# Attention of a gated linear mixer between the tiles of a projection, and modulation rows fetched tile by tile

## The reference

```python
# modulation: nine vectors of 1024 per layer
mod = c_act @ mod_w[l] + mod_b[l]
# gated linear mixer, layer 0 of the second block
xa, ga, q, k, v, g, za = split(u @ w_in)
ya = rg_lru(causal_conv(xa)) * gelu(ga)
log_alpha = log_sigmoid(za @ gla_wa2 + gla_ba) / 16
bc = cumsum(log_alpha over each chunk of 64 tokens)
q_dec, k_inv, k_end = q * exp(bc), k * exp(-bc), k * exp(b_last - bc)
scores = tril(q_dec @ k_inv.T)                    # inside a chunk
state = decay * state + k_end.T @ v               # from chunk to chunk
o = scores @ v + q_dec @ state
yb = rms_norm(o, gla_norm_g) * silu(g)
out = concat(ya, yb) @ w_out
```

## Time and profile before

| what | value |
|---|---|
| median of 3 runs | 3293.67 us (3288.68 to 3298.96) |
| the profiled execution | 3289.53 us, span 3287.7 us, mean granted PE clock 0.957 |
| busy: PE / DVE / ACT / POOL | 3010.6 / 1896.7 / 564.0 / 197.4 us |
| p2, 16 tiles | 2281.3 to 2336.5 us of the span |
| attention, outside of dense tiles | 2336.5 to 2399.0 us |
| pout | 2399.0 to 2456.1 us |
| small FFN without rows, first product to last | 211.6 us (2469.3 to 2680.9) |
| the four with rows | 218.6, 213.8, 214.1, 215.8 us |

### The profile page before, as it was taken

The page is one execution under the profiler, slowest core; times in us unless marked ns, Lnnn a source line. Parts: engine busy times, 40 slices in busy tenths (PEclk is TensorE's granted clock), DMA queues, the critical chain, the costliest instruction groups (busy, mean ns, idle before and its releaser), DMA issues.

```text
span 3287.7 us, 60931 instructions
## 1 busy us (share of the span) xinstructions
PE 3010.6 (92%) x26800; PEld 2580.0 (78%) x26800; DVE 1896.7 (58%) x3378; ACT 564.0 (17%) x1284; POOL 197.4 (6%) x315
## 2 busy tenths in 40 slices
PE   7999999777878899999899999999889999989998
PEld 6444444666667699999789999988769989976898
DVE  1777666543445377677547767744126656633674
ACT  1000001343233210100221010024101011022201
POOL 0000000331143000000000000000000000000000
PEclk8999999898999999999999999999799999998999
DMA  5668995101200446556424655634333535521453
GB/s 216 236 230 326 373 339 201 40 4 58 86 16 4 167 154 225 198 206 220 151 94 165 199 198 181 203 100 128 102 103 129 174 127 175 174 74 59 146 182 101
DMA packets 362050, 514.85 MB, mean 157 GB/s; under 512 B 10865, under 2 KB 349873, under 8 KB 352193
## 3 DMA queue, kind: packets, MB, share of 16 engines
q1 hardware_dynamic: 350992, 364.11, 34.2%
q0 software_dynamic: 10224, 144.18, 11.2%
q10 hardware_dynamic: 576, 2.75, 0.2%
HBM read 509.97 MB, written 1.05 MB: 155 GB/s over the span
## 4 chain that ended last, share of the span: by engine, by line
PE 81%; DMA 7%; DVE 4%; ACT 4%; issue 2%; POOL 1%; SPq 0%; DVEq 0%; ACTq 0%; POOLq 0%
PE PS L2424 25%; PE PS L2464 14%; PE PS L580 9%; PE PS L2354 7%; PE PS L2374 5%; PE PS L600 5%; PE PS L752 4%; DMA W<-in_ffn_w_gu 3%; PE PS L2333 2%; PE PS L2475 2%; DMA ADAW<-in_ada_rows 2%; DVE ADAW L2655 1%; PE PS L1327 1%; PE PS L1421 1%; PE PS L1552 1%
## 5 line engine op out<-in xcount | busy, mean ns | idle before, releaser
L2424 PE MATMUL PS<-Y,W 128*128 128x128 f32 x4928 | 594.9, 280 | 56.5 <-ACT Y L2577 32.0
L2424 PEld LDWEIGHTS PS<-Y,W 128*128 128x128 f32 x4928 | 577.3, 196 | 64.2 <-issue 34.4
L2424 PE MATMUL PS<-Y,ARENA 128*128 128x128 f32 x3696 | 438.7, 275 | 0.0
L2424 PEld LDWEIGHTS PS<-Y,ARENA 128*128 128x128 f32 x3696 | 426.0, 192 | 0.0
L2354 PE MATMUL PS<-Y,W 128*128 128x512 f32 x704 | 303.8, 594 | 2.2 <-DVE Y L2877 2.2
L2464 PE MATMUL PS<-ARENA,W 128*128 128x128 f32 x2464 | 286.1, 275 | 1.3 <-DVE ARENA L2761 0.7
L2464 PEld LDWEIGHTS PS<-ARENA,W 128*128 128x128 f32 x2464 | 280.2, 192 | 2.7 <-DVE ARENA L2761 2.7
L2354 PEld LDWEIGHTS PS<-Y,W 128*128 128x128 f32 x704 | 134.2, 191 | 171.0 <-issue 170.5
L2655 DVE SCALAR_TENSOR_TENSOR ADAW<-ADAW,CB 128x1024 f32<-128x1024 f32 x200 | 238.5, 1220 | 27.4 <-DMA ADAW<-in_ada_rows 27.0
L580 PE MATMUL PS<-Y,W 128*128 128x256 f32 (+2 forms) x816 | 184.8, 390 | 21.6 <-DMA W<-in_o_w_in 11.1
L580 PEld LDWEIGHTS PS<-Y,W 128*128 128x128 f32 (+2 forms) x816 | 157.3, 194 | 48.8 <-DMA W<-in_o_w_in 11.5
(11 more groups left out here) (395 smaller groups left out, 3617.7 us busy)
## 6 DMA issues: line engine op xcount, KB each, us to landing
ADAW<-in_ada_rows POOLq DMA_DIRECT2D x68, 2048.0 KB, 8.9
W<-in_ffn_w_gu SPq DMA_DIRECT2D x88, 1024.0 KB, 7.8
W<-in_ffn_in SPq DMA_DIRECT2D x88, 1024.0 KB, 7.6
W<-in_ffn_w_down SPq DMA_DIRECT2D x32, 1408.0 KB, 10.5
W<-in_ffn_out SPq DMA_DIRECT2D x32, 1408.0 KB, 8.6
W<-in_even_w_in SPq DMA_DIRECT2D x40, 512.0 KB, 4.7
W<-in_e_w_in SPq DMA_DIRECT2D x34, 512.0 KB, 4.7
ARENA<-in_ada_columns SPq DMA_DIRECT2D x4, 2048.0 KB, 24.9
```

Of the source, the lines that this page charges most:

```text
L2424: last = mm(block_bank(b, q), w[left][:, k, q * P:(q + 1) * P], YB[right][:, k], start=(k == 0 and p not in (2, 5)), stop=(k == 3), skip_g ...
```

## The change

In the gla mixer:
- The attention has its own counters (s_gm products done, s_ge products read, s_gz parts of Z16 ready) and its own banks 4 to 7 (`gbank`).
- p2 does the Gelu gates first. Its 16 tiles are written out one by one, and parts of the attention follow single tiles, by the table `beside`: scores and transposes after tile 0, the states of heads 0 to 3 after tiles 2 to 5, two outputs each after tiles 6 to 9, the two sums of squares after tiles 10 and 11. The square is done in two halves, the roots after tiles 11 and 12.
- ACT does the exponentials after value tile 4 (they stood after value tile 7) and the root of TH after the first p2 tile (it stood after value tile 6).
- DVE does the cumulative sums and differences ahead of TH, then the decayed q and k, then the RG-LRU product and scans, and doesn't wait for p2 before the attention.
- pout waits part by part for Z16: one count for the first eight blocks, then one for each of the others.
- ST lies where QG, KG and LA lay, RR where XAP and TH lay.

In the FFNs: a list `fetch` spreads the four tiles of each row group over the chunks from the one after group g-2's use up to the one ahead of its own. POOL issues each tile as a DMA of 0.5 MB (`row_tile`) when the chunk's products begin. The first two groups of F[1] and all groups before them are fetched whole, as before. `ada` waits for the sum of the four.

```diff
@@ in gla_phases, pe
-                proj_pe(pe, mm, m["p2"], lambda i: lambda k: Y[:, k, 0:S])
...
+                def tile(i):
+                    c, idx = sec["w0"] + i // 2, sec["t0"] + i
+                    pe.wait_ge(s_w[c % 2], 32 * (c // 2 + 1))
+                    pe.wait_ge(s_ev, idx - 3)
...
+                def scores():
+                    pe.wait_ge(s_xr, n_qk)
...
+                def states(h):
+                    pe.wait_ge(s_ge, G_ST)
                     for par in range(2):
-                        pe.wait_ge(s_ev, idx - 3)
+                        j = G_ST + 2 * h + par
+                        if j > 3:
+                            pe.wait_ge(s_ge, j - 3)
...
+                def output(i):
+                    j = G_OUT + i
+                    h, q = i // 2, i % 2
+
+                    pe.wait_ge(s_ge, max(G_ST + 2 * (h + 1), j - 3))
...
+                def square_sums(g):
+                    j = G_SQ + g
+                    pe.wait_ge(s_ga, squared + g)
+                    pe.wait_ge(s_ge, j - 3)
...
+                beside = {0: [(scores, ()), (keys_turned, ())], 2: [(states, (0,))], 3: [(states, (1,))],
+                          4: [(states, (2,))], 5: [(states, (3,))], 6: [(output, (0,)), (output, (1,))],
+                          7: [(output, (2,)), (output, (3,))], 8: [(output, (4,)), (output, (5,))],
+                          9: [(output, (6,)), (output, (7,))], 10: [(square_sums, (0,))], 11: [(square_sums, (1,))]}
+                for i in range(16):
+                    tile(i)
+                    for part, args in beside.get(i, ()):
+                        part(*args)
+                pe.wait_ge(s_ev, m["p2"]["t1"])
...
+                    for k in range(16):
+                        if i == 0 and k in (0, *range(DT, 16)):
+                            pe.wait_ge(s_gz, max(1, k - DT + 2))
@@ in gla_phases, act
-                    elif i == 6:
-                        act.wait_ge(s_xr, n_th)
-                        A(TH, TH, ACT.Sqrt).then_inc(s_ga, 1)
-                    elif i == 7:
+                    elif i == 4:
                         act.wait_ge(s_xr, n_be)
                         A(QD, BC, ACT.Exp)
...
+                    elif i == 8:
+                        act.wait_ge(s_xr, n_th)
+                        A(TH, TH, ACT.Sqrt).then_inc(s_ga, 1)
+                    elif i == 18:
+                        for g in range(2):
+                            act.wait_ge(s_ge, G_SQ - 4 + 4 * g)
+                            A(AI[:, 4 * g:4 * g + 4], AR_[:, 4 * g:4 * g + 4], ACT.Square).then_inc(s_ga, 1)
+                    elif i in (19, 20):
+                        g = i - 19
+                        act.wait_ge(s_gm, G_SQ + g + 1)
...
@@ in gla_phases, dve
-                dve.wait_ge(s_ga, 6)
-                link(V.tensor_scalar(YH, TH, 1.0, None, ALU.add))
-                link(V.reciprocal(YH, YH))
-                say(V.scalar_tensor_tensor(TH, TH, 2.0, YH, ALU.mult, ALU.mult), n_th)
...
-                dve.wait_ge(s_ga, 8)
+                dve.wait_ge(s_ga, 6)
+                link(V.tensor_scalar(YH, TH, 1.0, None, ALU.add))
+                link(V.reciprocal(YH, YH))
+                say(V.scalar_tensor_tensor(TH, TH, 2.0, YH, ALU.mult, ALU.mult), n_th)
+                dve.wait_ge(s_ga, 9)
+                V.tensor_tensor(QD, QD, QG, ALU.mult)
+                V.tensor_tensor(KI, KI, KG, ALU.mult)
+                say(V.tensor_tensor(KE, KE, KG, ALU.mult), n_qk)
+                link(V.memset(SCO, 0.0))
+                dve.wait_ge(s_ga, 10)
                 link(V.tensor_tensor(AI, AI, TH, ALU.mult))
                 for f in range(DT):
                     ins = V.tensor_tensor_scan(XC[:, f], AR_[:, f], AI[:, f], 0.0, ALU.mult, ALU.add)
...
-                dve.wait_ge(s_ev, m["sc"])
-                link(V.tensor_tensor(Z16[:, 0:DT], Z16[:, 0:DT], XC, ALU.mult))
...
+                dve.wait_ge(s_ev, m["p2"]["t0"] + DT)
+                V.tensor_tensor(Z16[:, 0:DT], Z16[:, 0:DT], XC, ALU.mult).then_inc(s_gz, 1)
+                dve.wait_ge(s_ga, squared + 3)
                 link(V.reciprocal(RR, RR))
...
                 for i in range(DT):
+                    dve.wait_ge(s_ev, m["p2"]["t0"] + DT + i + 1)
+                    V.scalar_tensor_tensor(Z16[:, 8 + i], AR_[:, i], vec("gla_norm_g_2", i % 2), Z16[:, 8 + i],
+                                           ALU.mult, ALU.mult).then_inc(s_gz, 1)
@@ ahead of the phases, and in POOL's program
+        chunk_uses = [used for sec in F[1:] for used in sec["groups"]]
+        used_in = [u for u, used in enumerate(chunk_uses) if used]
+        fetch = [[] for _ in chunk_uses]
+        for g, last in enumerate(used_in[2:], 2):
+            free_at = used_in[g - 2] + 1
+            for i in range(GROUP):
+                fetch[free_at + i * (last - free_at) // GROUP].append((F[1]["group0"] + g, i))
...
+            def row_tile(g, i):
+                pool.wait_ge(s_acc, g - 1)
+                pool.dma_start(ADAW[:, g % 2, i], t["ada_rows"][g * P:(g + 1) * P, i * D:(i + 1) * D])\
+                    .then_inc(s_adaw[g % 2], 16)
+
             def small_ffn(sec):
-                for g in range(sec["group0"] + 2, min(sec["group0"] + sum(sec["groups"]) + 2, len(ADA_GROUPS))):
-                    rows(g)
+                for u in range(PAIRS + 4):
+                    for g, i in fetch[(PAIRS + 4) * sec["i"] + u]:
+                        pool.wait_ge(s_mm, sec["t0"] + 7 * u)
+                        row_tile(g, i)
```

More of the change, by code:

```diff
@@ L1555, in pe @@
                         idx += 1
-                proj_pe(pe, mm, m["p2"], lambda i: lambda k: Y[:, k, 0:S])
-                idx = m["sc"]
-                pe.wait_ge(s_ev, idx)
-                pe.wait_ge(s_xr, n_qk)
-                for h in range(4):
-                    for c in range(4):
-                        tok = slice(c * HD, (c + 1) * HD)
-                        a = (h * 2 + c // 2) * HD
-                        last = mm(PS[idx % 4][(c % 2) * HD:(c % 2 + 1) * HD, a:a + HD], KI[:, h, tok], QD[:, h, tok],
-                                  start=True, stop=True)
@@ new lines, in tile @@
+                def tile(i):
+                    c, idx = sec["w0"] + i // 2, sec["t0"] + i
+                    pe.wait_ge(s_w[c % 2], 32 * (c // 2 + 1))
+                    pe.wait_ge(s_ev, idx - 3)
+                    for k in range(DT):
+                        last = mm(PS[idx % 4][:, 0:S], wide(c, DT)[:, k, (i % 2) * P:(i % 2 + 1) * P], Y[:, k, 0:S],
+                                  start=(k == 0), stop=(k == DT - 1))
+                    last.then_inc(s_mm, 1)
+                def scores():
+                    pe.wait_ge(s_xr, n_qk)
+                    for h in range(4):
+                        for c in range(4):
+                            tok = slice(c * HD, (c + 1) * HD)
+                            a = (h * 2 + c // 2) * HD
+                            last = mm(gbank(0)[(c % 2) * HD:(c % 2 + 1) * HD, a:a + HD], KI[:, h, tok], QD[:, h, tok],
+                                      start=True, stop=True)
+                    last.then_inc(s_gm, 1)
@@ L1599, in pe @@
[L1599 to L1600 removed]
+                        last.then_inc(s_gm, 1)
+                def output(i):
+                    j = G_OUT + i
+                    h, q = i // 2, i % 2
+                    pe.wait_ge(s_ge, max(G_ST + 2 * (h + 1), j - 3))
+                    v = slice(h * S + q * P, h * S + (q + 1) * P)
+                    for c in range(4):
+                        o = gbank(j)[:, c * HD:(c + 1) * HD]
+                        last = mm(o, VTOK[:, c // 2, v], SCO[:, h, c], start=True, stop=(c == 0))
+                        if c:
+                            last = mm(o, ST[:, h, c - 1, q * P:(q + 1) * P], QD[:, h, c * HD:(c + 1) * HD],
+                                      start=False, stop=True)
+                    last.then_inc(s_gm, 1)
@@ L2643, in ada @@
                 layer, tile = ADA_GROUPS[g]
-                if part[0] == 0:
+                g1 = F[1]["group0"] + 2
+                if part[0] == 0 and g < g1:
                     dve.wait_ge(s_adaw[g % 2], 16 * (g // 2 + 1))
+                elif g >= g1:
+                    whole = (g1 + 1 - g % 2) // 2
+                    dve.wait_ge(s_adaw[g % 2], 16 * (whole + GROUP * ((g - g1) // 2) + GROUP))
                 for i in part:
```

120 lines of the change are left out of this document (44 added, 76 removed).

## The result

The changed kernel took **3244.82 us** (median of 4 runs, 3241.72 to 3246.99), the kernel before 3292.34 on the same chip (4 runs, 3288.68 to 3298.96). The ratio is 0.9853, with a 95% interval of 0.9834 to 0.9871. The forecast was 3252, with a range of 3238 to 3268. The profiled execution has a span of 3245.2 us against 3287.7, 42.5 less where the sum said 41.7.

A forecast was written before the change was run, and what follows sets the result against it. PE dominates the chain (81% of the span), so only its idle or slow-clock time pays. Mixer 32.6 and fetches 9.1 (13.3 - 5.2 + 1.0) take 41.7 off 3289.5: 3247.8, median forecast 3252, range 3238 to 3268.

The forecast's parts named there:

- Step 1, the scores: Gla mixer after p2's tile 0: PE waits 5.5 us for DVE's n_qk, the clock falls, and the restart costs 1.9.
- The rival of late scores: Gla mixer: scores come as late as before, PE waits 8.7 us more; 3260 us, chance 0.03.
- Step 2, the two that meet: Gla mixer, before the states: PE arrives at 2301.3, DVE finishes at 2301.8, so PE waits 0.5 us.
- Step 3: Gla mixer, from the states to p2's end: states, outputs, square sums, remaining tiles and the square's wait, 65.2 us in all.
- The rival of a low clock in the outputs: Gla mixer: the clock stays low in the attention outputs, costing 18.9 us; 3271 us, chance 0.08.
- Step 4: Output projection after p2: starts 1.2 us later, waiting for weights, takes 55.3 us at full clock; DVE's 12.36 us tail is hidden.
- The fetches, gate/up: Small FFNs: with at most two 0.5 MB tiles beside a gate/up chunk, 13.3 us of PE's weight waits go.
- the rule that would have said so: DMA engines alternate queues by packet, so shorter-run tiles delay weights less; down-chunk loss nearer 2.6 than 5.2; not adopted.
- The fetches, the down chunks: Small FFNs, first down chunk: tiles delay weights and DVE's sums; one uncovered tile per FFN, 5.2 us lost, 7.8 at worst.
- The conv mixer: Start of conv, an 11.13 us PE weight wait: without the 2 MB row fetch ahead, 1.0 us gained (ends 0 and 5.2).
- The sum: Whole kernel: 32.6 us from the gla mixer plus 9.1 from the row fetches, 41.7 off the profiled execution, giving 3247.8.
- Slower: Gla mixer: the scores' wait drops the clock and it stays low until the output projection; 3323 us, chance 0.03.

The follow-up runs named there:

- outputs_block: Changed kernel, with all eight attention outputs in one block after p2 tile 9 instead of in pairs after tiles 6 to 9; 3245.68 us.
- four_at_once: Changed kernel, with all four tiles of a row group issued together at the first chunk start where their buffer is free; 3241.46 us.
- whole_at_start: Changed kernel, with each row group fetched by one 2 MB DMA at the same chunk starts as in four_at_once; 3255.69 us.
- off_chunk10: Changed kernel, with the row tiles that fell beside gate/up chunk 10 moved to the first down chunk; 3239.35 us.
- lump_at_conv: Changed kernel, with the row group before conv held back and its four tiles issued together when the second FFN is done; 3249.65 us.
- before_kept_busy: Kernel before, with twelve unused 128x256 products filling PE's wait ahead of the attention's states; 3284.66 us.
- before_kept_busy2: Kernel before, with twelve unused 128x256 products ahead of the states and 2, 2, 3 and 5 more behind the four heads' states; 3281.05 us.

## Why the prediction was right, and where its steps were wrong

- **Step 1, the scores.** Wait 5.45 us against 5.5, ended by the product of n_qk as worked out. The clock fell as expected; the scores, transposes and tiles 1 and 2 took 11.84 us against 6.9 + 1.9 + 2.3 = 11.1. The rival of late scores falls.
- **Step 2, the two that meet.** DVE's key copies ended at 2288.61, PE reached the states at 2289.03: no wait, where I had 0.5.
- **Step 3.** States 4.2 us against 3.5, outputs 12.3 against 12.1, wait for the square 1.4 against 1.3. Square sums 1.99 + 1.73 = 3.7 against 3.4. The largest mis-sized term is the tiles: one takes 3.65 or 3.51 us when a part follows it, not 3.45, which makes 1.0 in 13. p2 with everything took 88.3 us against 85.7: 1.0 for the tiles, 0.7 each for step 1 and the states, 0.6 for outputs, sums and the square, less the 0.5 of step 2. The mixer still gave only 1.7 less than forecast, because the part ahead of p2, which the sum didn't touch, took 1.1 less than before (101.6 against 102.7); that is scatter, and luck. The rival of a low clock in the outputs falls, and outputs_block shows that tiles between the pairs are not needed for that.
- **Step 4.** pout started 1.2 us after p2, as forecast, and took 55.49 against 55.3. The profile puts the wait down to ACT's last eviction (L1686), but that ended 0.8 us earlier. The weights that I named fit: the first chunk was issued at 2349.71, the second half some 0.4 later, and landed after 7.6 at 2357.8; no run tests it. No wait for Z16 appeared.
- **The fetches, gate/up.** 13.3 us of waits gone, as said, but for the wrong reason: the number was right by luck. The step "the lump cost its neighbour 5.2, so one tile costs 1.3" priced bytes. four_at_once keeps the bytes beside the chunk and has 0.9 us; whole_at_start puts them back into one DMA and has 13.5. I weighed the rule that would have said so and kept to the rows; the rows held only lumps, so they couldn't tell bytes from the length of a run.
- **The fetches, the down chunks.** 7.1 us more of waits (7.8 against 0.7 in all) for a forecast of 5.2, in all four FFNs and from the two waits named (W and DVE's sums). off_chunk10 shows that these tiles cause it. The rule's 2.6 for this term was the worse guess: tiles of 4 KB runs too cost something where nothing is slack.
- **The conv mixer.** 3.2 us instead of 1.0. The step that failed is "it is nearly through before the weights start": it took the delay that the lump causes, 5.2, for the time that it lasts. In the kernel before the lump of 1586.52 lands after 8.3 us, 2.7 after W's first issue, and that issue itself is slow beside it. lump_at_conv, with tiles ahead of W by the same 5.6 us, still loses 2.9.
- **The sum.** 1.7 too much for the mixer, 2.6 too little for the rest; they nearly cancel, by luck. The named waits make 13.3 - 7.1 + 3.2 = 9.4 us of the 11.7; the other 2.3 are in none of them, and are no more than the restarts scatter by. For the profiled execution the sum gave 3247.8, and it took 3246.99. The 7 us between the forecast of 3252 and the median of 3244.8 are the step from the profiled execution to the median: I added 4.1, as for the kernel before, but the changed kernel's profiled execution is the longest of its four, 2.2 over their median.
- **Slower.** The mechanism needed a clock that tiles don't bring back. In the changed kernel they did from 2283.07 on, behind the scores; the narrow products of the attention didn't, in 25 us (before_kept_busy).

## What to carry to other kernels

Put small dependent products with banks and counters of their own between dense tiles, each behind the tile by which its producer is done; that hides the waits, and it keeps the clock that the waits would cost, which was at least a third of the mixer's gain. If a background transfer delays weights, try to cut it into smaller DMAs with shorter runs before you move its date: at the same bytes and chunk starts the waits went from 13.5 to 5.0 to 0.9 us, while the date alone gave nothing. Leave such transfers away from chunks that are larger than their neighbours, and let the first weights of a stage be issued ahead of its small tables.

## What the hardware showed that I had not expected

- Products of 64 columns kept 2.4 GHz when it was granted as they began (outputs_block and before_kept_busy2, 12 to 13 us of them), and didn't raise 1.2 GHz in 25 us (before_kept_busy), at a PE that is recorded busy in all three. Full tiles (128x256) raised it in both kernels: in pout of before, and in p2 of the changed kernel from 2283.07 on.
- In before_kept_busy the clock fell after three waits of 0.8, 0.3 and 1.7 us among short products; with these waits filled too (before_kept_busy2) it didn't.
- How one transfer is cut changed when another one landed (14.4, 12.9, 10.3 us), with the time at which both are through the same within 0.9 us.
- SP's four weight issues took 2.69 us alone, and 5.40 and 5.72 beside a group of rows.
- The same stage, with the same waits, can be 3 us longer from one execution to the next, by how long the slow clock lasts after a pause (0.50 or 0.88 in the same 10 us window of FFN1; 2.5 us in the mixer's first projection). A single execution can't price an edit under some 5 us; the waits in it can.
